# A hybrid decoder step: small loads first, modulations as whole rows, and gathers and scatters that follow the token count

## The reference, cut to what matters

```
sh_m, sc_m, g_m, sh_f, sc_f, g_f = split(silu(c) @ ada_w + ada_b, 6)     # 9 conditioning rows, 6 x 1024 columns
xn = rmsnorm(x, norm_mix_g) * (1 + sc_m) + sh_m
x  = x + g_m * mixer(xn)             # w_in (1024 x 2048): xa, ga, u, v; LRU beside a spatial gate; w_out (1024 x 1024)
xn = rmsnorm(x, norm_ffn_g) * (1 + sc_f) + sh_f
scores = sigmoid(xn @ router_w)      # 64 experts, the best 8 of each token
x  = x + g_f * (sum over the 8 experts of gate * (silu(xn@Wg) * (xn@Wu)) @ Wd  +  shared expert)
y  = rmsnorm(x, final_norm_g)
```

## Time and profile before

| | |
|---|---|
| median of 3 runs | 897.2 us (896.88 to 899.55) |
| the profiled execution | 903.51 us, its span 901.7 us |
| busy: PE, POOL, DVE, ACT | 726.1, 391.9, 327.3, 226.0 us |
| granted clock of PE, mean | 0.909 of full speed |
| moved by DMA | 279.31 MB in 87888 packets, mean 310 GB/s |
| first L1019 of the experts, end of PE's last expert product | 267.11 us, 854.55 us |

### The profile page before, as it was taken

How to read it: one execution, slowest core, us unless ns; L and a number is a source line. 1 busy time by engine, 2 the same in 40 slices (tenths; PEclk the granted TensorE clock), 3 DMA queues, 4 the chain that set the end, 5 groups by cost and what they waited for, 6 DMA issues and landing times.

```text
span 901.7 us, 14433 instructions
## 1 busy us (share of the span) xinstructions
PE 726.1 (81%) x5084; PEld 407.4 (45%) x5085; DVE 327.3 (36%) x610; ACT 226.0 (25%) x384; POOL 391.9 (43%) x319
## 2 busy tenths in 40 slices
PE   2686999998879877998798889897889778898900
PEld 2564656445535434554454545454455334454400
DVE  3105275455613344323232332333333323233306
ACT  4102532022022231223222222222232222233202
POOL 0000102011442756566565565466656455476223
PEclk9796999998789997999899989999899988898955
DMA  9997759437317999999999999999999999899143
GB/s 276 389 354 272 269 195 336 159 121 302 140 41 284 395 402 399 354 372 394 399 390 383 375 371 366 373 359 390 406 372 370 379 362 352 284 386 380 15 89 136
DMA packets 87888, 279.31 MB, mean 310 GB/s; under 512 B 30059, under 2 KB 33707, under 8 KB 62872
## 3 DMA queue, kind: packets, MB, share of 16 engines
q1 hardware_dynamic: 51970, 250.40, 71.0%
q0 software_dynamic: 30752, 25.94, 12.8%
q10 hardware_dynamic: 5110, 2.24, 1.0%
HBM read 285.39 MB, written 39.15 MB: 360 GB/s over the span
## 4 chain that ended last, share of the span: by engine, by line
PE 37%; DMA 34%; issue 11%; DVE 6%; ACTq 4%; POOL 3%; SPq 2%; ACT 2%; POOLq 1%; DVEq 0%
DMA acc_rows<-et,idx 20%; PE bank L1019 9%; PE bank L1055 7%; DMA et<-xn_rows,idx 7%; DMA xn<-xn_rows,idx 5%; PE bank L793 4%; PE bank L902 3%; PE bank L785 2%; DMA gu<-in_ada_w 2%; PE bank L765 2%; DVE et L1492 2%; PE bank L1004 2%; ACTq L576 1%; POOL acc_rows L476 1%; POOL acc_rows L481 1%
## 5 line engine op out<-in xcount | busy, mean ns | idle before, releaser
L1019 PE MATMUL bank<-gu,et 128*64 128x256 f32 x2496 | 284.4, 383 | 4.9 <-ACT et L681 2.9
L1019 PEld LDWEIGHTS bank<-gu,et 128*64 128x64 f32 x2496 | 182.2, 139 | 131.3 <-issue 51.7
L476 POOL DMA_INDIRECT acc_rows<-et,idx x64 | 103.9, 1624 | 197.2 <-DVE et L1492 174.4
L1055 PE MATMUL bank<-dn,et 128*64 128x512 f32 x624 | 171.0, 682 | 11.9 <-issue 9.8
L481 POOL DMA_INDIRECT acc_rows<-et,idx x64 | 101.9, 1593 | 19.5 <-issue 18.6
L1492 DVE TENSOR_SCALAR et<-bank,mb 128x512 f32<-128x512 f32 x64 | 48.0, 751 | 169.6 <-DMA acc_rows<-et,idx 125.7
L696 ACT ACTIVATE et<-bank,mb 128x512 f32<-128x512 f32 x64 | 44.0, 688 | 231.1 <-DMA acc_rows<-et,idx 162.2
L1055 PEld LDWEIGHTS bank<-dn,et 128*64 128x64 f32 x624 | 43.7, 150 | 88.1 <-issue 88.1
L1485 DVE COPY et<-bank 128x256 f32<-128x256 f32 x64 | 27.1, 423 | 144.1 <-PE bank L1036 108.6
L1471 DVE COPY et<-bank 128x512 f32<-128x512 f32 x64 | 44.2, 691 | 84.1 <-PE bank L1004 78.2
L688 ACT ACTIVATE et<-bank 64x512 f32<-64x512 f32 x64 | 37.8, 590 | 142.0 <-PE bank L1019 117.3
(11 more groups left out here) (264 smaller groups left out, 619.5 us busy)
## 6 DMA issues: line engine op xcount, KB each, us to landing
gu<-in_exp_w_gate SPq DMA_DIRECT2D x64, 1024.0 KB
gu<-in_exp_w_up SPq DMA_DIRECT2D x64, 1024.0 KB
dn<-in_exp_w_down SPq DMA_DIRECT2D x64, 1024.0 KB
gu<-in_ada_w SPq DMA_DIRECT2D x12, 2048.0 KB, 15.0
gu<-in_w_in SPq DMA_DIRECT2D x4, 2048.0 KB, 19.1
gu<-in_w_out SPq DMA_DIRECT2D x2, 2048.0 KB, 16.8
acc_rows<-dn SPq DMA_DIRECT2D x2, 1280.0 KB, 15.0
acc_rows<-et,idx POOLq DMA_INDIRECT x128
```

The source lines that it names most:

```text
L476: pool.indirect_dma_start(acc_rows[u % 2], bass.IndirectOffsetOnAxis(ap=idx[:, u, 0:1], axis=0), yo[:, u % 2, 0, :], None, bounds_check=2 ...
L1019: mm = pe.matmul(bank[u % 2][64 * c:64 * c + 64, b * FE:(b + 1) * FE], xt[:, b, k % 4, k // 4, :], w[:, (c * KT + k) * FE:(c * KT + k + 1) ...
L1055: mm = pe.matmul(bank[5 + b][64 * c:64 * c + 64, :], hT[:, b, j, :], dn[:, dslot(u), j * D + c * HALF:j * D + (c + 1) * HALF], start=(j == ...
```

## The change

Four parts; the lines of the changed kernel are some ten to twenty higher.

1. **Small loads.** ACT issues 26 small transfers at the head of its queue, ahead of the squaring of x: channel rows, norm gain and spatial-gate bias as rows (PE turns them, which replaces three kinds of transfers of single elements), the bias of the first two modulations (`adam`), the gate matrices, the other biases and norm_ffn_g. The spatial-gate weights, two rows and the router go to SP's queue between pieces, eight small blocks of the spatial gate to POOL's.
2. **Modulations.** The first four pieces are now 256 rows of 8 KB, two of the eight k-slices with all 2048 columns of both modulations. PE sums them over the four pieces in one bank (`mix`, 8 products of 512 columns per piece), then come one addition, four turns and four coefficient instructions. The sample tokens' scaling goes from POOL to DVE; of the prompt's, DVE takes k=0 to 2 and ACT 3 to 7.
3. **Routing.** `turn("z", 0)` stands between `wout(1)` and `wout(2)`; tile 1's shared product is cut 2, 3, 3 in place of 4, 4.
4. **Branches.** POOL reads the expert's count in `gather` and in `scatter`. Only a full expert issues the second gather and the second scatter; any other issues a transfer of 4 bytes in its place, which counts on the same semaphore.

```diff
-        PIECES = ([("ada", j) for j in range(4)] + [("in", 0), ("ada", 4), ("ada", 5), ("in", 1), ("ada", 6), ("ada", 7),
+        PIECES = ([("mix", j) for j in range(4)] + [("in", 0), ("ada", 4), ("ada", 5), ("in", 1), ("ada", 6), ("ada", 7),
...
+            if kind == "mix":
+                return s["mix_used"], j + 1
...
+                return s["mod_ready"], j - 3
...
+        skipped = small[0:1, 24:24 + 2 * U]
...
-                if n == 1:
-                    bsrc = io["ada_b"].rearrange("o (j g n) -> o j g n", j=12, g=4)
...
-                if n == 3:
-                    sync.dma_start(gnT, io["norm_mix_g"][0].rearrange("(k p) -> p k", p=P)).then_inc(s["ld_gnT"], 16)
...
+                if n == 6:
+                    sync.dma_start(wnat, io["sgu_w"][0].rearrange("g p q -> p g q")).then_inc(s["ld_sgu"], 16)
...
+                    sync.dma_start(vg_row, io["sgu_norm_g"].to_broadcast([P, W])).then_inc(s["ld_rows"], 16)
...
+                    sync.dma_start(wrt[:, :, :], io["router_w"][0].rearrange("(p k) e -> p k e", k=KT)).then_inc(s["ld_router"], 16)
...
+                if kind == "mix":
+                    sync.dma_start(guf[n % SLOTS].rearrange("p (k n) -> p k n", k=2), mix_p[:, 2 * j:2 * j + 2, 0:2 * D]).then_inc(ld_piece[n % SLOTS], 16)
...
-            pool.tensor_tensor(xTs, xTs, over_t(mixA), ALU.mult).then_inc(s["mix_s"], 1)
...
+            for b in range(NB):
+                pool.dma_start(wsn[8 * b:8 * b + 8, :, 8 * b:8 * b + 8],
+                               io["sgu_w"][0, :, 0:NT, 0:NT].rearrange("g p q -> p g q")).then_inc(s["ld_wsn"], 16)
...
+            def is_full(r, i, u):
+                return pool.value_load(cnt_i[0:1, bass.ds(i * U + u, 1)], min_val=0, max_val=T) > (r * ROUND + 64)
...
+                full = is_full(r, i, u)
-                pool.indirect_dma_start(xg[u % XB][:, 1, :], None, xn_half,
-                                        bass.IndirectOffsetOnAxis(ap=idx[:, u, 1:2], axis=0),
-                                        bounds_check=2 * T - 1, oob_is_err=False).then_inc(gathered2[u % XB], 16)
+                with pool.If(full):
...
+                with pool.Else():
+                    pool.dma_start(skipped[:, u:u + 1], halfc[0:1, :]).then_inc(gathered2[u % XB], 16)
...
+                full = is_full(r, i, u)
...
-                pool.indirect_dma_start(acc_rows[u % 2], bass.IndirectOffsetOnAxis(ap=idx[:, u, 1:2], axis=0),
...
+                with pool.If(full):
...
+                with pool.Else():
+                    pool.dma_start(skipped[:, U + u:U + u + 1], halfc[0:1, :]).then_inc(scattered[u % 2], 16)
...
+            for r0, src in rows:
+                act.dma_start(chrow[r0:r0 + src.shape[0], :], src).then_inc(s["ld_ch"], 16)
             act.wait_ge(s["ld_c"], 32)
             act.activation(crow, crow, ACT.Silu).then_inc(s["csilu"], 1)
+            act.dma_start(gbrow[0:8], io["norm_mix_g"][0].rearrange("(k p) -> k p", p=P)).then_inc(s["ld_gb"], 16)
+            act.dma_start(gbrow[8:16], io["sgu_b"][0]).then_inc(s["ld_gb"], 16)
+            act.wait_ge(s["adab_zero"], 1)
+            for j in range(4):
+                act.dma_start(adam[32 * j:32 * j + NSEQ], io["ada_b"][:, 512 * j:512 * (j + 1)].to_broadcast([NSEQ, 512])).then_inc(s["ld_adam"], 16)
+            act.wait_ge(s["blk_zero"], 3)
+            for wt, name in ((wr, "gate_r_w"), (wi, "gate_i_w")):
+                for h in range(2):
+                    act.dma_start(wt[64 * h:64 * h + 64, :, 64 * h:64 * h + 64],
+                                  io[name][0].rearrange("(c h) i j -> h i c j", h=2)[h]).then_inc(s["ld_rg"], 16)
...
+            act.wait_ge(s["gnf_zero"], 2)
+            for g in range(4):
+                act.dma_start(adab[32 * g:32 * g + NSEQ, 4:12], bsrc[:, 4:12, g, :].to_broadcast([NSEQ, 8, P])).then_inc(s["ld_adab"], 16)
+                act.dma_start(gnf[32 * g:32 * g + NSEQ], gsrc[:, :, g, :].to_broadcast([NSEQ, 2, P])).then_inc(s["ld_gnf"], 16)
...
             act.wait_ge(s["ld_x"], 32)
             act.wait_ge(s["sumsq_v"], 2)
...
+            act.wait_ge(s["mix_coef"], 4)
...
+            for k in range(3, KT):
...
-            for r0, src in rows:
-                act.dma_start(chrow[r0:r0 + src.shape[0], :], src).then_inc(s["ld_ch"], 16)
-            act.dma_start(wnat, io["sgu_w"][0].rearrange("g p q -> p g q")).then_inc(s["ld_sgu"], 16)
...
-            for b in range(NB):
...
-                              io["sgu_w"][0, :, 0:NT, 0:NT].rearrange("g p q -> p g q")).then_inc(s["ld_wsn"], 16)
...
-            act.dma_start(og_row, io["out_norm_g"][:, W:2 * W].to_broadcast([P, W])).then_inc(s["ld_rows"], 16)
-            act.dma_start(bsT, io["sgu_b"][0].rearrange("g p -> p g")).then_inc(s["ld_rows"], 16)
-            for b in range(NB):
-                act.dma_start(bsS[8 * b:8 * b + 8, :], io["sgu_b"][0, :, 0:NT].rearrange("g p -> p g")).then_inc(s["ld_rows"], 16)
-            act.dma_start(wrt[:, :, :], io["router_w"][0].rearrange("(p k) e -> p k e", k=KT)).then_inc(s["ld_router"], 16)
-            act.dma_start(rbias[:, :], io["router_bias"].to_broadcast([P, NE])).then_inc(s["ld_router"], 16)
...
-            pe.wait_ge(s["tp_evac"], 1)
+            pe.wait_ge(s["ld_gb"], 32)
+            pe.wait_ge(s["sel_in"], 1)
+            pe.transpose(tp_wait("gb")[:, 0:16], gbrow, ident[0:16, 0:16]).then_inc(s["tp_ready"], 1)
+            pe.wait_ge(s["tp_evac"], TP["gb"] + 1)
+            pe.matmul(tp_wait("bs")[0:64, 0:8], sel, bsT[0:8, :], start=True, stop=True).then_inc(s["tp_ready"], 1)
...
-            def turn_mod(j):
-                pe.wait_ge(s["mod_evac"], j + 1)
-                pe.transpose(bank[4][:, j * P:(j + 1) * P], mods[:, j, :], ident[:, :]).then_inc(s["modT_ready"], 1)
...
-            ada(0)
+            def mix(n):
+                w = piece("mix", n).rearrange("p k n -> p (k n)")
+                for k in range(2):
+                    for j in range(4):
+                        mm = pe.matmul(bank[0][32 * j:32 * j + 32, :], cT[:, 2 * n + k, :],
+                                       w[:, k * 2 * D + j * 512:k * 2 * D + (j + 1) * 512], start=(n == 0 and k == 0), stop=(n == 3 and k == 1))
+                mm.then_inc(s["mix_used"], 1)
+
+            mix(0)
             turn("x", "xn_done", 0)
-            ada(1)
+            mix(1)
             turn("x", "xn_done", 1)
             turn("x", "xn_done", 2)
-            ada(2)
-            turn_mod(0)
-            turn_mod(1)
-            ada(3)
-            turn_mod(2)
-            turn_mod(3)
+            mix(2)
+            mix(3)
+            pe.wait_ge(s["mod_evac"], 4)
+            for q in range(4):
+                mm = pe.transpose(bank[4][:, q * P:(q + 1) * P], mods[:, q, :], ident[:, :])
+            mm.then_inc(s["modT_ready"], 1)
+            pe.wait_ge(s["mix_s"], 2)
             pe.wait_ge(s["mix_s"], 2)
...
             wout(1, range(4, KT))
+            turn("z", "xn_ready", 0)
             wout(2, range(4, KT))
...
-            turn("z", "xn_ready", 0)
             pe.wait_ge(s["tp_evac"], TP["z01"] + 1)
...
-            tile_product(bank[5], 1, gu[SH_SLOT], 2 * FE, range(4))
+            tile_product(bank[5], 1, gu[SH_SLOT], 2 * FE, range(2))
             pe.wait_ge(s["tp_evac"], TP["z21"] + 1)
             logits(2)
+            tile_product(bank[5], 1, gu[SH_SLOT], 2 * FE, range(2, 5))
...
-            tile_product(bank[5], 1, gu[SH_SLOT], 2 * FE, range(4, KT)).then_inc(s["sh_ready"], 1)
+            tile_product(bank[5], 1, gu[SH_SLOT], 2 * FE, range(5, KT)).then_inc(s["sh_ready"], 1)
...
-                mod(j)
...
+            dve.wait_ge(s["ld_adam"], 64)
+            dve.wait_ge(s["mix_used"], 4)
+            dve.tensor_tensor(mods[:, 0:4, :].rearrange("p j n -> p (j n)"), bank[0][:, :], adam, ALU.add).then_inc(s["mod_evac"], 4)
...
+            for j in range(2):
+                dve.scalar_tensor_tensor(mixA[:, 4 * j:4 * j + 4, :], modT[:, 1, j, :, 0:NSEQ], 1.0,
+                                         gnT[:, 4 * j:4 * j + 4].rearrange("p (k o) -> p k o", o=1).to_broadcast([P, 4, NSEQ]),
+                                         ALU.add, ALU.mult).then_inc(s["mix_coef"], 1)
+                dve.tensor_copy(mixB[:, 4 * j:4 * j + 4, :], modT[:, 0, j, :, 0:NSEQ]).then_inc(s["mix_coef"], 1)
...
-            for k in range(4):
...
+            dve.tensor_tensor(xTs, xTs, over_t(mixA), ALU.mult).then_inc(s["mix_s"], 1)
+            dve.wait_ge(s["mix_s"], 1)
+            dve.tensor_tensor(xTs, xTs, over_t(mixB), ALU.add).then_inc(s["mix_s"], 1)
+            for k in range(3):
                 dve.tensor_scalar(xT[:, k, 0:NPR], xT[:, k, 0:NPR], mixA[:, k, 0:1], mixB[:, k, 0:1], ALU.mult, ALU.add).then_inc(s["mix_v"], 1)
```

More of the change, by code:

```diff
@@ L95, in build @@
         mixB = iota_s[:, 72:144].rearrange("p (k q) -> p k q", k=KT)
-        gnT = iota_s[:, 144:152]
+        gbT = iota_s[:, 144:160]
+        sel = iota_s[0:8, 160:224]
+        gnT, bsT = gbT[:, 0:8], gbT[:, 8:16]
```

(2 more changed lines are left out.)

90 lines of the change are left out of this document (41 added, 49 removed).

## The result

The changed kernel takes 867.96 us (median of four runs, 864.97 to 869.71), the kernel before 898.38 in the same set: a ratio of 0.9646, 95% interval 0.9616 to 0.9675. The medians lie 30.4 us apart, the ratio gives about 32. In a second set on one chip the ratio was 0.9613 (0.9583 to 0.9642). Forecast were 859 us and a gain of 38, range 841 to 884. The two profiled executions, 903.51 and 867.74, lie 35.8 us apart, since that of before lies at the upper end of its four runs, 896.88 to 903.82.

The account below looks back on a forecast made before the run. The weight stream was taken to bound the experts for 562 us, with PE behind because gathers land late. Start -13, routing -4, stream -10 and tail -11 sum to -38: 897.2 - 38 = 859 us, range 841 to 884.

Parts of the forecast that it names:

- Two of its own signs: Start and experts: the forecast would be wrong if squares start past 20; q0 should have near 18000 packets.
- The start: From kernel start to the second input product: ACT's late issues and PE's 12.14 us wait go, -13 us.
- the other 14 lie between these two prices, 3.9 to 20.3, and I take 6: Head of ACT's queue: 14 of the 26 small loads ahead of the squares cost 6 us together.
- Rival B: Head of ACT's queue: 26 loads take 27 us, squares near 30, start gains 0; 872 us in all, chance 0.14.
- The routing: Routing: tile 0's earlier turn and the 2, 3, 3 cut of the shared product give -4 us.
- The experts: Expert loop: skipping second gathers and scatters gives -21 us, -10 from the stream and -11 from PE's backlog.
- the weight stream sets the pace for 562 us: Expert loop, 272 to 834 us: DMA share 1.00 at 373 GB/s was taken to mean the weight stream bounds.
- PE falls behind because gathers land late: Expert loop: PE, about three experts behind at the stream's end, waits 64.4 us at turns of gathered rows.
- Its -10 for packets: Expert loop: removing 100 of 256 indirect transfers takes 10 us off the 562 us stream; ends 0 and 19.
- Its -11 for the tail: After the weight stream's end: PE stays within two experts of it, 17 us where 28 stand; ends 0 and -18.
- Rival A: Expert loop gives nothing, DMA being at 1.00 throughout; only start and routing, -17, remain: 880 us, chance 0.17.
- Rival C: Expert loop: POOL becomes the bound through 3.7 us per guard (count read and branch); slower, 1060 us, chance 0.07.

## Why the prediction was right, and where not

The total, its sign and the range held; the gain was 30 to 32 us where 38 were forecast. That the differences are the same for the profiled execution and the median did not hold: the traces differ by 36. Two of its own signs spoke against it: the squares started past 20, and q0 has 23008 packets for near 18000, since against its stand-in a dropped scatter counts 112 packets and a dropped gather 48 (5600 and 2400 over 50), not 128 each. By its own steps:

- **The start failed in one term,** "the other 14 lie between these two prices, 3.9 to 20.3, and I take 6". They took 20: 0.7 us for the two gain rows, 1.6 for four bias rows, 17.9 for the last eight. (The four gate transfers took 2.7 for 5.8.) Rival B had the place right and its time of the squares, 30 against 27.17; only its end differs, since xa came 5 us earlier than it had it: from the turned x to xa it allowed 11 us, and the trace has 7.6. The gap before the second product closed as forecast, with the table load and evacuation between.
- **The routing** was forecast at -4; its order gave 7.6 us at equal clock in the output product, some 5 of them apart from the clock around the mask. The -10.0 of the table is these 7.6, less 2.5 for the clock's fall in the output product of that one trace, and another 5 from the granted clock earlier on, a term the prediction did not have. The windows of before, then of after:

```profile
64.00:76.00 12.00, 0.19 (x8) 0.00 (x0) 0.21 (x2) 1.80 (x4) 0.66 (x1) 0.67 1.09 363
76.00:97.00 21.00, 20.67 (x85) 14.19 (x89) 13.00 (x51) 4.72 (x12) 3.75 (x6) 0.86 0.49 171
207.00:224.00 17.00, 13.04 (x69) 8.59 (x68) 8.06 (x27) 4.50 (x11) 1.98 (x4) 0.83 0.75 307
224.00:235.00 11.00, 11.00 (x50) 5.71 (x50) 5.34 (x22) 0.00 (x0) 2.51 (x5) 0.79 0.07 10
```

```profile
68.00:72.00 4.00, 4.00 (x133) 3.75 (x133) 2.83 (x17) 2.78 (x10) 0.00 (x0) 1.00 0.65 198
72.00:89.00 17.00, 17.00 (x64) 11.91 (x64) 10.96 (x39) 2.02 (x4) 2.27 (x4) 1.00 1.00 354
200.00:213.00 13.00, 12.46 (x73) 8.00 (x72) 8.35 (x29) 4.45 (x10) 1.99 (x4) 1.00 1.01 423
213.00:221.00 8.00, 8.00 (x50) 4.60 (x48) 5.52 (x21) 0.00 (x0) 2.99 (x5) 1.00 0.48 145
```

PE idled 12 us before the second product; the clock was 0.67 of full speed there and 0.86 in the product, which took 20.16 us. Now PE has no gap, the clock is 1.00, the product takes 17.50: 2.7 us. Around the mask PE idled some 4 of 17 us, and the clock was 0.83 and then 0.79; now 1.00. This part belongs to the order: with it undone the clock is 0.78 there again (213 to 225). (1.00 is the upper of its two levels, 2.4 GHz; a mean below is a mixture with the lower, 1.2.) In the run with the order undone the first four slices of tile 1's shared product take 3.70 us, before 5.28: another 1.6 of the 5.

```profile
211.69 5.28 PE L793 MATMUL bank<-gu,xT 128*128 128x512 f32 x8
```

- **The experts** came out at -20.3 for -21, but "the weight stream sets the pace for 562 us" was wrong. The DMA share of 1.00 misled. It is 1.02 at 401 GB/s as it is 1.00 at 373, and says only that something is in flight. PE released slots late, "PE falls behind because gathers land late" was right, and with the waits at gathered rows gone the weights are what PE waits for. So the gain is the distance between two limits, the gathers' chain at 590 us and the stream at 570, and not a sum of a stream term and a tail. The step that failed is this sum. Its -10 for packets was too much: engine time of q0 fell by 6.3 us, the 8-byte packets' part is 4.5, and with 5600 of 8000 packets back the stretch grew by 2. The upper end of that term, 19 us by transfers, charged dropped rows with more than they have: in the trace before all 8-byte packets together hold 9.8 of q0's 115.4 us. Its -11 for the tail stands or falls with where the stream ends: read at the last row of weights, the stream is 6 us shorter and the tail 24 - 9 = 15; read at 795, they are 24 shorter and 4 longer. That -10 and -11 met -20.3 is luck.
- **Rival A** rested on the same reading, that a full stream leaves nothing to win; its other half, that dropped rows cost the engines little, was nearly true (4.5 us), and yet they held the gathers. The upper end of the range, 884 as "A with half the routing", should have been 882.
- **Rival C** is refuted for this kernel by the run that branches and skips nothing.

What stays open: by which steps late scatters and late gathers hand the delay to each other, and why it costs 2 us with 5600 of the packets back and 18 with 8000. Each guard alone removes nearly all of it, so the chain passes through both; the runs don't show the links one by one. PE's own busy time in the stretch fell too, from 510.65 to 502.06 us at a clock of 0.97 for 0.94; no run separates that from the waits.

## What to carry to other kernels

A DMA share of 1.00 says that something is always in flight, not that the stream is the bound; look at the time from issue to landing of the prefetched loads, and at which wait PE ends. Rows in a queue that shares its engines with long rows can cost more than the 9 ns that they take, even if they are dropped: here 17 us of stretch for 4.5 us of engine time. Take them out where a count is at hand, and expect a limit, not a sum. Before a few us are put down to a change of order, compare the granted clock of the stretch in both traces. Issue small loads early only as far as the queue takes them at 0.3 us; behind that, put them past the work of the engine that issues them.
